# Hybrid decoder layer with a 32-expert MoE on one core: the gather reads the residual, not its normalised copy, and the router's steps are reordered

## The chip, the core and the metric

The kernel runs on one core of one Trainium2 chip. The metric is the device time of one execution in microseconds. The time before the change is the median of three runs, 1175.53 us (1170.3 to 1177.52).

## What is computed

One decoder layer over 256 positions of width 1024, all in f32: a mixer with 8 mLSTM heads and 8 attention heads, a top-4-of-32 MoE, and a gated per-layer embedding. The change touches the MoE and what stands ahead of it. Cut to that:

```python
def rmsnorm(x, g):
    return x * lax.rsqrt(jnp.mean(x * x, axis=-1, keepdims=True) + 1e-6) * g

x = x + mix @ w_out                                   # x2 in the kernel
t = rmsnorm(x, ffn_norm_g)                            # (256, 1024)
logits = t @ w_router + b_router                      # (256, 32)
top_vals, top_idx = lax.top_k(logits, 4)
gates = sum(one_hot(top_idx, 32) * softmax(top_vals)[..., None], axis=1)
for e in range(32):
    hu = t @ w_gate_up[e] + b_gate_up[e]              # 1024 -> 2 * 1024
    glu = jnp.minimum(hu[:, :1024], 7.0)
    lin = jnp.clip(hu[:, 1024:], -7.0, 7.0)
    y = y + gates[:, e:e + 1] * ((glu * sigmoid(1.702 * glu) * (lin + 1.0)) @ w_down[e] + b_down[e])
x = x + y
x = x + sigmoid(rmsnorm(x, ple_norm_g) @ w_ple_gate) * (p @ w_ple_proj)
```

## The kernel before

The kernel is one program with the order of every engine written out by hand. SP (the sync engine) issues all DMAs, PE does the matmuls, DVE, ACT and POOL the rest, and semaphores tie them together. Positions are held as two tiles `tt` of 128 rows. `xt` is the residual, 128 x 2 x 1024. A quadrant `q` is tile `q // 2`, columns `q % 2` times 512. PSUM has eight banks: `hu` (4), `po` (2) and `aux` (2).

**Weights.** They stream through `ring`, nine slots of 2 MB. `chunk_done` counts the chunks that PE has used up. Nine chunks for the mixer come first; chunk 9 of that count is the end of the output projection. The MoE then takes 192 chunks: per pair of experts 12 (`STREAM`), four of `w_gate_up` for the first expert, one for the second, two of `w_down` for the first, and so on. The first nine MoE chunks (m = 0 to 8) are loaded ahead as slots come free, m = 8 only when the router's partial products of both tiles are in PSUM (`lpart_ps`, L407). Chunk m = 9 and all later ones are refills: SP waits until PE has done chunk m - 9 (L409), and then loads 2 MB.

**From the mixer to the first gather.** PE adds the output projection in `hu`, quadrant by quadrant. DVE adds each to `xt` (`residual`, L1101), PE transposes the quadrant (L754), ACT squares it for the norm (L1441) and copies the transposed one (L1447). From these PE makes partial logits (`logit_parts`, L762), which ACT copies out (L1453), and then logits (L769). DVE routes a tile (`route_tile`, L1167 to L1178): scaled logits, the top 8, a mask of the chosen experts. PE counts positions by matmuls with the mask (L788, L790, L802), DVE turns them into slot numbers (`positions`, L1184) and a one-hot matrix of the pair's two experts with 64 slots each (L1186). `tile_h2` (L1158) writes the normalised rows h2 = xt x root x g_ffn, stored with the columns permuted. The gather multiplies h2 (the stationary operand, 128 x 128 contiguous) with the one-hot matrix into `aux` (first one: L795), and ACT copies the result to `xg` (L1473). The order of these steps on DVE is: residual 0, 1, root and h2 of tile 0, residual 2, 3, routing of tile 0, root of tile 1, positions of tile 0, h2 of tile 1, routing and positions of tile 1.

**The loop.** It runs over 16 pairs, in one pass of 64 slots where no expert has more rows. PE in a pair: first up chunk (`up_block`, L843; after its first half of k the bias, L835), scatter of the pair before in two tiles (L828, added to `xt` by DVE, L1246) between the next chunks, transposes of the gated one-hot (L900), the remaining up chunks of expert 0 and the first of expert 1, the transposes of the activation (L850), down projection (L864), three up chunks of expert 1, the gather for the next pair (L819, 16 matmuls of two passes each), transposes, down projection. DVE makes `sel`, the gated one-hot, the next one-hot (L1220) and the activations (L1260 to L1266).

**After the loop.** The last scatter, the transposes of `xt`, the gate projection (L973) and the output, which is built in `xs` (L1318, L1320). `h2` and `xs` are the same memory, `big1`.

## Time and profile before

| | |
|---|---|
| median of three runs | 1175.53 us (1170.3 to 1177.52) |
| the profiled execution, whole | 1174.7 us |
| its span, first to last instruction | 1172.6 us |
| granted TensorE clock, mean of the span | 0.989 |
| PE busy | 1124.6 us (96%) |
| DVE busy | 235.5 us (20%) |
| ACT busy | 159.9 us (14%) |
| POOL busy | 19.6 us (2%) |
| read from HBM | 429.51 MB, 367 GB/s over the span |
| chain that ended last | PE 70%, DMA 27%, DVE 1%, ACT 1% |

The profile is one execution. Times are in us from the span's start unless they are called ns. PE is the matmul side of TensorE and PEld its weight loads, which overlap it. An f32 matmul shows as two records, one per pass. The chain of work is followed back from the last instruction, each time to what released it. The granted clock is a share of 2.4 GHz. L-numbers are lines of the kernel; those of the new kernel are about 15 to 23 higher in the same place.

### The profile page before, as it was taken

What the parts mean: (1) busy time and instruction counts of PE and PEld (TensorE: products, weight loads), DVE (VectorE), ACT (ScalarE), POOL (GpSimd) and SP (SyncE); (2) the same over time, 40 slices, a digit from 0 to 9 for tenths busy, and PEclk for the clock granted to TensorE, in tenths of its full rate; (3) what the DMA queues carried; (4) which work ended last, traced back from release to release, by engine and by line L of the source; (5) the groups of instructions that cost most, each with busy time, mean ns of one, the idle gap of its engine ahead of it and who ended that gap; (6) DMA issues with size and microseconds to landing.
All of it is one profiled execution on the core that took longest, in us unless ns stands there. A gap on an engine that the chain in (4) does not pass through costs nothing.

```text
span 1172.6 us, 12150 instructions
## 1 busy us (share of the span) xinstructions
PE 1124.6 (96%) x5234; PEld 454.4 (39%) x5234; DVE 235.5 (20%) x480; ACT 159.9 (14%) x304; POOL 19.6 (2%) x44
## 2 busy tenths in 40 slices
PE   6999997999999999999999999899989998999998
PEld 3476544343434343433343333333333332424243
DVE  2364134202111111112121111111111110202021
ACT  3223312100101000000011010000000000101031
POOL 2000110000000000000000000000000000000000
PEclk9999988999999999999999999999999999999999
DMA  9932416699999999999999999999999999999950
GB/s 338 328 135 81 161 73 268 258 430 427 427 428 429 426 427 429 428 427 428 428 425 428 427 428 428 428 428 427 427 428 428 428 426 426 428 428 428 426 211 36
DMA packets 41214, 431.36 MB, mean 368 GB/s; under 512 B 5728, under 2 KB 5984, under 8 KB 16584
## 3 DMA queue, kind: packets, MB, share of 16 engines
q1 hardware_dynamic: 41160, 430.57, 87.8%
q8 instruction: 42, 0.69, 0.2%
q14 instruction: 12, 0.10, 0.0%
HBM read 429.51 MB, written 1.05 MB: 367 GB/s over the span
## 4 chain that ended last, share of the span: by engine, by line
PE 70%; DMA 27%; DVE 1%; ACT 1%; SPq 0%; issue 0%; POOL 0%; POOLq 0%; DVEq 0%; ACTq 0%
DMA ring<-in_w_gate_up 26%; PE hu L843 24%; PE po L864 14%; PE hu L542 5%; PE aux L819 5%; PE aux L828 3%; PE hu L548 2%; PE hu L557 2%; PE hu L835 2%; PE po L856 2%; PE po L973 1%; PE hu L973 1%; PE po L850 1%; PE aux L795 1%; PE po L681 0%; PE po L900 0%
## 5 line engine op out<-in xcount | busy, mean ns | idle before, releaser
L843 PE MATMUL hu<-ring,xg_t 128*64 128x512 f32 x2048 | 466.6, 597 | 22.6 <-DMA ring<-in_w_gate_up 22.6
L843 PEld LDWEIGHTS hu<-ring,xg_t 128*64 128x64 f32 x2048 | 137.7, 136 | 329.0 <-issue 284.4
L864 PE MATMUL po<-ring,early 128*64 128x512 f32 x1024 | 226.8, 595 | 0.0
L864 PEld LDWEIGHTS po<-ring,early 128*64 128x64 f32 x1024 | 70.7, 137 | 153.9 <-issue 131.4
L1260 DVE TENSOR_SCALAR early<-hu 128x512 f32<-128x512 f32 x32 | 22.1, 692 | 462.7 <-PE hu L843 462.7
L1246 DVE TENSOR_TENSOR xt<-xt,aux 128x512 f32<-128x512 f32 x68 | 43.7, 685 | 164.2 <-PE aux L828 164.2
L542 PE MATMUL hu<-ring 128*128 128x512 f32 x160 | 71.0, 597 | 0.0
L828 PE MATMUL aux<-num_t,early 64*128 64x512 f32 x272 | 67.6, 615 | 0.3 <-ACT num_t L1493 0.3
L819 PEld LDWEIGHTS aux<-early,big 128*128 128x128 f32 x512 | 58.4, 192 | 13.0 <-issue 13.0
L819 PE MATMUL aux<-early,big 128*128 128x128 f32 x512 | 61.4, 278 | 0.0
L1485 ACT ACTIVATE early<-early 128x512 f32<-128x512 f32 x32 | 20.2, 630 | 253.1 <-DVE early L1260 253.1
L1493 ACT COPY num_t<-po 128x512 f32<-128x512 f32 x32 | 18.8, 586 | 238.1 <-PE po L864 238.1
L1496 ACT COPY early<-po 128x512 f32<-128x512 f32 x16 | 9.4, 586 | 248.1 <-PE po L900 248.1
L542 PEld LDWEIGHTS hu<-ring 128*128 128x128 f32 x160 | 29.6, 190 | 34.9 <-issue 34.5
L828 PEld LDWEIGHTS aux<-num_t,early 64*128 64x128 f32 x272 | 23.5, 186 | 43.2 <-issue 42.4
L835 PE MATMUL hu<-bias,early 32*64 32x512 f32 x256 | 34.8, 613 | 0.0
L856 PE MATMUL po<-bias,early 32*64 32x512 f32 x128 | 34.4, 613 | 0.0
L557 PE MATMUL hu<-ring 128*128 128x512 f32 x64 | 33.5, 675 | 0.0
L1270 DVE COPY early<-sel_part 128x128 f32<-128x128 f32 x16 | 3.6, 228 | 142.0 <-PE po L864 140.9
L548 PE MATMUL hu<-ring 128*128 128x256 f32 x128 | 29.8, 386 | 0.0
L1489 ACT COPY early<-po 128x512 f32<-128x512 f32 x32 | 18.8, 589 | 62.6 <-PE po L850 62.6
L548 PEld LDWEIGHTS hu<-ring 128*128 128x128 f32 x128 | 23.7, 190 | 5.4 <-DVE ring L1089 1.7
(242 smaller groups left out, 549.6 us busy)
## 6 DMA issues: line engine op xcount, KB each, us to landing
ring<-in_w_gate_up SPq DMA_DIRECT2D x128, 2048.0 KB, 34.5
ring<-in_w_down SPq DMA_DIRECT2D x64, 2048.0 KB, 36.8
ring<-in_w_in SPq DMA_DIRECT2D x7, 2048.0 KB, 15.0
ring<-in_w_out SPq DMA_DIRECT2D x2, 2048.0 KB, 8.2
ring<-in_w_ple_gate SPq DMA_DIRECT2D x2, 2048.0 KB, 35.9
xt<-in_x SPq DMA_DIRECT2D x2, 512.0 KB, 4.0
ring<-in_w_ple_proj SPq DMA_DIRECT2D x1, 1024.0 KB, 33.2
out_x<-big SPq DMA_DIRECT2D x4, 256.0 KB, 2.0
```

The source lines that it names most:

```text
L542: last = mm(bank, hT[:, k, tt * P:(tt + 1) * P], slot(n, NB, K)[:, k, :], start=(k == 0), stop=(k == K - 1))
L548: last = mm(bank[:, 0:S], slot(n, NB, K)[:, k, ct * P:(ct + 1) * P], hT[:, k, :], start=(k == 0), stop=(k == K - 1))
L557: last = mm(hu[:, q, :], mixT[:, k, tt * P:(tt + 1) * P], slot(n, D, 4)[:, k % 4, b * NB:(b + 1) * NB], start=(k == 4), stop=(k == 3))
L819: last = mm(aux[:, c, (k % 4) * P:(k % 4 + 1) * P], h2[:, tt, k * P:(k + 1) * P], onehot[:, tt, :, :].rearrange("p e s -> p (e s)"), start ...
L828: last = mm(aux[:, n, :], ghotT[r, e, tt * P:(tt + 1) * P], out_s[r, e, :], start=(e == 0), stop=(e == 1))
L835: mm(hu[n * SLOTS:(n + 1) * SLOTS, 2 * e + b, :], sel[32 * b:32 * b + E, e * SLOTS:(e + 1) * SLOTS], bias[32 * b:32 * b + E, n * NB:(n + 1 ...
L843: last = mm(hu[n * SLOTS:(n + 1) * SLOTS, 2 * e + b, :], xg[:, k, e * SLOTS:(e + 1) * SLOTS], w[:, o:o + NB], start=(k == 0), stop=(k == K ...
L856: mm(po[n * SLOTS:(n + 1) * SLOTS, 0, :], sel[64:64 + E, e * SLOTS:(e + 1) * SLOTS], bias[64:64 + E, n * NB:(n + 1) * NB], start=True, sto ...
L864: last = mm(po[n * SLOTS:(n + 1) * SLOTS, 0, :], actT[:, f, h * SLOTS:(h + 1) * SLOTS], w[:, o:o + NB], start=False, stop=(h == 1 and f == ...
L973: last = mm(QUAD_BANKS[q], x3T[:, k, tt * P:(tt + 1) * P], final_slot(1 + k // 4, D, 4)[:, k % 4, n * NB:(n + 1) * NB], start=(k == 0), st ...
L1246: v.tensor_tensor(quad(xt, q), quad(xt, q), aux[:, n, :], ALU.add).then_inc(y_done, 1)
L1260: v.tensor_scalar(glu, hu[:, 2 * e, :], LIMIT, None, ALU.min).then_inc(glu_ready, 1)
```

## The change

The gather now takes `xt` itself as the stationary operand. `x_rows(tt, k)` picks every eighth column, so its 128 columns lie 8 floats apart, where h2 was read contiguously. The factor 1 / rms of each row goes into the one-hot matrix (`one_hot_tile`: one tensor_scalar per expert, compare and multiply, where one tensor_tensor did both experts), and g_ffn, now 128 x 8 in `g_perm`, is multiplied in where the gathered rows leave PSUM (`gathered`, now on DVE, 128 x 512 from PSUM, twice per pair; it was a copy on ACT). The scatter's one-hot would hold that factor too, so the gates are multiplied by the rms. `tile_h2` and the load of g_ffn over all partitions (512 KB) are gone.

The first gather writes to banks 2 and 3 of `hu`, and tile 0's half of it stands before tile 1's counting matmuls on PE. Since the gather reads `xt` in every pair, y can no longer be added there: the sums are kept in `ysum` (the memory that held h2), which POOL fills with four copies of `xt`, and the end of the kernel reads `ysum` where it read `xt`, and writes the output to `xt`.

The first refill (m = 9) is loaded in two halves, the first when PE has done the first block of chunk 0 (`first_free`). The bias matmuls of the up projection stand behind k = 2, in the second chunk, instead of behind k = 0.

```diff
-        g_ffn = sb("g_ffn", [P, D])
+        g_perm = sb("g_perm", [P, K])
...
-        h2 = xs
         hm = xs
+        ysum = xs
...
-                    sp.dma_start(g_ffn[:], ffn_norm_g.to_broadcast([P, D])).then_inc(late_loaded, 16)
+                    sp.dma_start(g_perm[:], ffn_norm_g.rearrange("o (p k) -> p (o k)", k=K)).then_inc(late_loaded, 16)
...
+                if m == RING:
+                    kind, e, part = STREAM[m]
+                    assert (kind, e) == (0, 1) and m < PER_PAIR
+                    sp.wait_ge(first_free, 1)
+                    sp.dma_start(ring[:, moe_slot(m), 0:2048], gu_src[1, part, :, 0:2048]).then_inc(first_half, 16)
+                    sp.wait_ge(chunk_done, MOE0 + 1)
+                    sp.dma_start(ring[:, moe_slot(m), 2048:4096], gu_src[1, part, :, 2048:4096])\
+                      .then_inc(ring_full[moe_slot(m)], 16)
+                    continue
...
             g.memset(ghotT, 0.0).then_inc(ghotT_ready, 1)
             g.memset(out_s, 0.0).then_inc(out_s_ready, 2)
+            for q in range(QUADS):
+                pool.wait_ge(x2_ready, q + 1)
+                g.tensor_copy(quad(ysum, q), quad(xt, q)).then_inc(y_init, 1)
...
-            def gather_part(tt, c, first):
+            def x_rows(tt, k):
+
+                return xt[:, tt, :].rearrange("p (q k) -> p k q", k=K)[:, k, :]
+
+            def first_gather(tt, c):
 
                 for k in range(4 * c, 4 * c + 4):
-                    last = mm(aux[:, c, (k % 4) * P:(k % 4 + 1) * P], h2[:, tt, k * P:(k + 1) * P],
-                              onehot[:, tt, :, :].rearrange("p e s -> p (e s)"), start=(first and k % 4 == 0), stop=not first,
+                    last = mm(hu[:, 2 + c, (k % 4) * P:(k % 4 + 1) * P], x_rows(tt, k),
+                              onehot[:, tt, :, :].rearrange("p e s -> p (e s)"), start=(tt == 0 and k % 4 == 0), stop=(tt == 1),
                               skip_group_check=True)
                 return last
 
+            pe.wait_ge(onehot_ready, 2)
+            for c in range(2):
+                first_gather(0, c)
             pe.wait_ge(mask_ready, 2)
             for b in range(2):
                 last = mm(po[:, 1, b * E:(b + 1) * E], (ones if b else before)[:], mask[:, 1, :], start=False, stop=True,
                           skip_group_check=True)
             last.then_inc(pos_ps, 1)
-            pe.wait_ge(onehot_ready, 1)
-            pe.wait_ge(xs_ready, TT + 1)
+            pe.wait_ge(onehot_ready, 4)
             for c in range(2):
-                gather_part(0, c, True)
-            pe.wait_ge(onehot_ready, 2)
-            pe.wait_ge(xs_ready, 2 * TT)
-            for c in range(2):
-                gather_part(1, c, False).then_inc(xg_ps, 1)
+                first_gather(1, c).then_inc(xg_ps, 1)
 
             def gather():
 
                 for c in range(2):
                     for k in range(4 * c, 4 * c + 4):
                         for tt in range(TT):
...
                         wait_moe_chunk(pe, ps, m)
+                        if m == RING:
+                            pe.wait_ge(first_half, 16)
                         for k in (2 * c, 2 * c + 1):
                             last = up_block(e, ring[:, moe_slot(m), :], k)
-                            if k == 0:
+                            if m == 0 and k == 0:
+                                last.then_inc(first_free, 1)
+                            if k == 2:
                                 pe.wait_ge(sel_ready, pairs + (pair + 1))
                                 up_bias(e)
                         last.then_inc(chunk_done, 1)
...
+            def one_hot_tile(tt, first):
+                for e in range(2):
+                    v.tensor_scalar(onehot[:, tt, e, :], iota_s[:], posm[:, tt, first + e:first + e + 1],
+                                    stat[:, 16 + TT + tt:17 + TT + tt], ALU.is_equal, ALU.mult).then_inc(onehot_ready, 1)
...
             residual(0)
             residual(1)
             tile_rstd(0)
-            tile_h2(0)
             residual(2)
             residual(3)
+            dve.wait_ge(lpart_ps, 1)
+            v.tensor_copy(lpart[:, 0:P], aux[:, 0, 0:P]).then_inc(lpart_ready, 1)
             route_tile(0)
             tile_rstd(1)
+            route_tile(1)
             positions(0)
-            tile_h2(1)
-            route_tile(1)
             positions(1)
 
-            def one_hot(first):
-                v.tensor_tensor(onehot, iota_s[:].rearrange("p (a b s) -> p a b s", a=1, b=1).to_broadcast([P, TT, 2, SLOTS]),
-                                posm[:, :, first].rearrange("p t (e o) -> p t e o", o=1).to_broadcast([P, TT, 2, SLOTS]),
-                                ALU.is_equal).then_inc(onehot_ready, 1)
+            def gathered(bank, count):
+
+                for c in range(2):
+                    dve.wait_ge(xg_ps, count + (c + 1))
+                    v.tensor_tensor(xg[:, 4 * c:4 * c + 4, :], bank[:, c, :].rearrange("p (k s) -> p k s", k=4),
+                                    g_perm[:, 4 * c:4 * c + 4].rearrange("p (k o) -> p k o", o=1).to_broadcast([P, 4, P]),
+                                    ALU.mult).then_inc(xg_ready, 1)
 
             routed(v.tensor_scalar(posm[:, :, E:E + 2], posm[:, :, 0:2], -float(SLOTS), None, ALU.add), False)
             routed(v.tensor_reduce(cnt[:, 0:1], po[:, 1, E:2 * E], AX.X, ALU.max), False)
...
+            gathered(hu[:, 2:4, :], 0)
...
-                v.tensor_scalar(gates[:, tt, :], gates[:, tt, :], stat[:, 36 + tt:37 + tt], None, ALU.mult)\
-                 .then_inc(gates_ready, 1)
+                v.tensor_scalar(gates[:, tt, :], gates[:, tt, :], stat[:, 36 + tt:37 + tt],
+                                stat[:, 8 + TT + tt:9 + TT + tt], ALU.mult, ALU.mult).then_inc(gates_ready, 1)
             dve.wait_ge(gates_ready, TT)
+            dve.wait_ge(y_init, QUADS)
...
-                    v.tensor_tensor(quad(xt, q), quad(xt, q), aux[:, n, :], ALU.add).then_inc(y_done, 1)
+                    v.tensor_tensor(quad(ysum, q), quad(ysum, q), aux[:, n, :], ALU.add).then_inc(y_done, 1)
...
                     activation(1)
-
-                dve.wait_ge(onehot_ready, pairs + (PAIRS + 2))
+                    gathered(aux[:], ps * (2 * PAIRS) + (2 * pair + 2))
...
-            def logit_rows(tt):
-
-                act.wait_ge(lpart_ps, tt + 1)
-                a.copy(lpart[:, tt * P:(tt + 1) * P], aux[:, tt, 0:P]).then_inc(lpart_ready, 1)
-
-            for q in range(QUADS):
+            for q in range(2):
                 act.wait_ge(x2_ready, q + 1)
-                quad_squares(q, 24 + q, junk)
-                if q == 1:
-                    root(TT, stat[:, 2:3], True)
-                if q == 3:
-                    logit_rows(0)
+                quad_squares(xt, q, 24 + q, junk)
+            root(TT, stat[:, 2:3], True)
+            for q in range(2):
+                quad_columns_x2(q)
+            for q in range(2, QUADS):
+                act.wait_ge(x2_ready, q + 1)
+                quad_squares(xt, q, 24 + q, junk)
                 quad_columns_x2(q)
             root(TT + 1, stat[:, 3:4], True)
-            logit_rows(1)
+            act.wait_ge(lpart_ps, 2)
+            a.copy(lpart[:, P:S], aux[:, 1, 0:P]).then_inc(lpart_ready, 1)
             for tt in range(TT):
                 act.wait_ge(negtop_ready, tt + 1)
                 a.activation(gates[:, tt, :], lg[:, tt, :], ACT.Exp, bias=stat[:, 32 + tt:33 + tt]).then_inc(route_exp, 1)
 
-            def gathered(count):
-
-                for c in range(2):
-                    act.wait_ge(xg_ps, count + (c + 1))
-                    a.copy(xg[:, 4 * c:4 * c + 4, :].rearrange("p k s -> p (k s)"), aux[:, c, :]).then_inc(xg_ready, 1)
-
-            gathered(0)
...
-                    gathered(ps * (2 * PAIRS) + (2 * pair + 2))
```

DVE, from the end of tile 0's routing to the logits of tile 1 (`lg`), `mask` and `posm` are the chosen experts and slot numbers, `big` is h2. Before:

```order
L1172 CAST topf<-topi 128x8
L1173 TENSOR_TENSOR early<-iota_e,topf 128x128
L1177 TENSOR_REDUCE mask<-early 128x32
L1178 TENSOR_SCALAR stat<-top 128x1
L1153 TENSOR_TENSOR stat<-stat 128x1
L986 RECIPROCAL stat<-stat 128x1
L1184 SCALAR_TENSOR_TENSOR posm<-po,mask 128x32
L1186 TENSOR_TENSOR early<-iota_s,posm 128x128
L1158 SCALAR_TENSOR_TENSOR big<-xt,stat,g_ffn 128x128x8
L1167 SCALAR_TENSOR_TENSOR lg<-aux,stat,brb 128x32
L1170 MAX top<-lg 128x8
L1171 MAX_INDEX topi<-top,lg 128x8
```

Now, from the same place; `early<-iota_s,posm,stat` is the one-hot with the root in it:

```order
L1174 TENSOR_TENSOR stat<-stat 128x1
L1007 RECIPROCAL stat<-stat 128x1
L1180 SCALAR_TENSOR_TENSOR lg<-aux,stat,brb 128x32
L1183 MAX top<-lg 128x8
L1184 MAX_INDEX topi<-top,lg 128x8
L1185 CAST topf<-topi 128x8
L1186 TENSOR_TENSOR early<-iota_e,topf 128x128
L1190 TENSOR_REDUCE mask<-early 128x32
L1191 TENSOR_SCALAR stat<-top 128x1
L1202 SCALAR_TENSOR_TENSOR posm<-po,mask 128x32
L1195 TENSOR_SCALAR early<-iota_s,posm,stat 128x64 x2
L1202 SCALAR_TENSOR_TENSOR posm<-po,mask 128x32
```

The second h2 has gone from between, and positions of tile 0 moved from ahead of tile 1's routing to behind it.

PE, from the last logits to the first gather; `po` rows are the counting matmuls, L795 the gather of both tiles. Before:

```order
L762 MATMUL aux<-ring,w_r 32x128 x8
L769 MATMUL aux<-sel_part,early 128x32
L788 MATMUL po<-mask,before 128x32
L790 MATMUL po<-mask,ones 128x32 x2
L802 MATMUL po<-mask,before 128x32
L802 MATMUL po<-mask,ones 128x32
L795 MATMUL aux<-early,big 128x128 x16
```

Now; L814 is the gather, into `hu`:

```order
L777 MATMUL aux<-ring,w_r 32x128 x8
L784 MATMUL aux<-sel_part,early 128x32
L803 MATMUL po<-mask,before 128x32
L805 MATMUL po<-mask,ones 128x32 x2
L814 MATMUL hu<-early,xt 128x128 x8
L824 MATMUL po<-mask,before 128x32
L824 MATMUL po<-mask,ones 128x32
L814 MATMUL hu<-early,xt 128x128 x8
```

Tile 0's eight gather matmuls moved ahead of tile 1's two counting ones (L824).

ACT, from the first square of the residual on (`early,stat<-xt` is a square, `ring<-hu` the copy of a transposed quadrant, `stat<-stat` a root, `early<-aux` the copy of partial logits). Before:

```order
L1441 ACTIVATE early,stat<-xt 128x512
L1447 COPY ring<-hu 128x4x128
L1441 ACTIVATE early,stat<-xt 128x512
L1331 ACTIVATE stat<-stat,eps_t 128x1
L1447 COPY ring<-hu 128x4x128
L1441 ACTIVATE early,stat<-xt 128x512
L1447 COPY ring<-hu 128x4x128
L1441 ACTIVATE early,stat<-xt 128x512
L1453 COPY early<-aux 128x128
L1447 COPY ring<-hu 128x4x128
L1331 ACTIVATE stat<-stat,eps_t 128x1
L1453 COPY early<-aux 128x128
```

Now:

```order
L1464 ACTIVATE early,stat<-xt 128x512 x2
L1354 ACTIVATE stat<-stat,eps_t 128x1
L1470 COPY ring<-hu 128x4x128 x2
L1464 ACTIVATE early,stat<-xt 128x512
L1470 COPY ring<-hu 128x4x128
L1464 ACTIVATE early,stat<-xt 128x512
L1470 COPY ring<-hu 128x4x128
L1354 ACTIVATE stat<-stat,eps_t 128x1
L1485 COPY early<-aux 128x128
```

The second square and the root moved ahead of the first copy, and the copy of tile 0's partial logits left ACT for DVE.

## Rows read from the trace of the kernel before

**Rows 1.** Page: GB/s in 40 slices of 29.3 us each.
```profile
GB/s 338 328 135 81 161 73 268 258 430 427 427 428 429 426 427 429 428 427 428 428 425 428 427 428 428 428 428 427 427 428 428 428 426 426 428 428 428 426 211 36
```

**Rows 2.** Windows: us, busy PE PEld DVE ACT POOL, clock, DMA, GB/s.
```profile
200.00:210.00 10.00, 8.93 (x44) 7.73 (x44) 4.43 (x23) 2.03 (x4) 0.00 (x0) 0.61 0.18 74
210.00:220.00 10.00, 10.00 (x48) 3.13 (x48) 1.28 (x2) 0.75 (x1) 0.00 (x0) 1.00 0.65 228
...
400.00:1100.00 700.00, 680.13 (x3350) 246.26 (x3352) 110.89 (x192) 63.74 (x109) 0.00 (x0) 1.00 1.01 427
```

**Rows 3.** Chain in order of time: start, length, what.
```profile
208.51 1.87 PE hu L843 x8
...
264.30 1.72 PE hu L843 x8
...
658.47 38.11 DMA ring<-in_w_gate_up
...
1072.28 38.43 DMA ring<-in_w_gate_up
...
1119.65 7.04 PE po L864 x32
```

**Rows 4.** Timeline of the DMA queue (SP): the first refills.
```profile
213.30 0.33 SPq L398 DMA_DIRECT2D ring<-in_w_gate_up  x1
218.80 0.33 SPq L398 DMA_DIRECT2D ring<-in_w_down  x1
224.30 0.33 SPq L398 DMA_DIRECT2D ring<-in_w_down  x1
228.47 0.33 SPq L398 DMA_DIRECT2D ring<-in_w_gate_up  x1
```

**Rows 5.** Timeline of the routing and first gather, PE, DVE and ACT.
```profile
186.37 1.88 PE L557 MATMUL hu<-ring 128*128 128x512 f32 x4
...
189.93 1.26 DVE L1101 TENSOR_TENSOR xt<-xt,hu 128x512 f32<-128x512 f32 x2
...
192.92 0.26 ACT L1453 COPY early<-aux 128x128 f32<-128x128 f32 x1
...
194.14 0.25 DVE L1167 SCALAR_TENSOR_TENSOR lg<-aux,stat,brb 128x32 f32<-128x32 f32 x1 [2.94 <-PE aux L769]
...
195.74 0.15 DVE L1153 TENSOR_TENSOR stat<-stat 128x1 f32<-128x1 f32 x1
...
196.13 0.25 ACT L1453 COPY early<-aux 128x128 f32<-128x128 f32 x1
...
199.40 0.23 DVE L1167 SCALAR_TENSOR_TENSOR lg<-aux,stat,brb 128x32 f32<-128x32 f32 x1
...
201.07 0.63 PE L802 MATMUL po<-mask,before 128*128 128x32 f32 x2 [3.56 <-DVE mask L1177]
...
201.94 6.56 PE L795 MATMUL aux<-early,big 128*128 128x128 f32 x32
...
202.39 0.29 DVE L1186 TENSOR_TENSOR early<-iota_s,posm 128x128 f32<-128x128 f32 x1
```

**Rows 6.** Timeline: POOL, product of two operands from SBUF.
```profile
164.55 1.04 POOL L488 TENSOR_TENSOR big<-big 128x512 f32<-128x512 f32 x1 [1.92 <-DVE big L1130]
```

**Rows 7.** PEld groups by line; timeline of PE for the same lines.
```profile
L819 PEld LDWEIGHTS aux<-early,big 128*128 128x128 f32 x512 | 58.4, 192 | 13.0 <-issue 13.0
...
L850 PEld LDWEIGHTS po<-ident,early 128*128 128x128 f32 x128 | 17.9, 207 | 13.0 <-issue 13.0
...
L900 PEld LDWEIGHTS po<-ident,early 128*128 128x128 f32 x64 | 6.7, 141 | 13.0 <-issue 13.0
```

**Rows 8.** Timeline of PE: transposes L900, gather L819, transposes L850.
```profile
224.19 0.66 PE L900 MATMUL po<-ident,early 128*128 128x128 f32 x4
...
251.97 3.84 PE L819 MATMUL aux<-early,big 128*128 128x128 f32 x32
...
255.64 0.64 PE L850 MATMUL po<-ident,early 128*128 128x128 f32 x4
```

More of the change, by code:

```diff
@@ L265, in hybrid_layer @@
         ghot_ready = sem("ghot_ready")
+        y_init = sem("y_init")
+        first_free = sem("first_free")
+        first_half = sem("first_half")
         ghotT_ps = sem("ghotT_ps")
@@ L427, in _ @@
                 sp.wait_ge(fin_step, 2 * q + 2)
-                sp.dma_start(quad(out_dst, q), quad(xs, q)).then_inc(stored, 16)
+                sp.dma_start(quad(out_dst, q), quad(xt, q)).then_inc(stored, 16)
             sp.wait_ge(stored, 16 * TT * HALVES)
@@ L749, in _, with quad_transposes @@
             w_out_part(3, range(0, 2))
-            def quad_transposes(q, bank):
+            def quad_transposes(src, q, bank):
                 for j in range(4):
-                    last = tr(bank[:, j * P:(j + 1) * P], quad(xt, q)[:, j * P:(j + 1) * P], ident[:])
+                    last = tr(bank[:, j * P:(j + 1) * P], quad(src, q)[:, j * P:(j + 1) * P], ident[:])
                 last.then_inc(xq_ps, 1)
@@ L780, in _ @@
             pe.wait_ge(x2_ready, 4)
-            quad_transposes(3, hu[:, 3, :])
+            quad_transposes(xt, 3, hu[:, 3, :])
             logits(0)
@@ L818, in gather @@
                         for tt in range(TT):
-                            last = mm(aux[:, c, (k % 4) * P:(k % 4 + 1) * P], h2[:, tt, k * P:(k + 1) * P],
+                            last = mm(aux[:, c, (k % 4) * P:(k % 4 + 1) * P], x_rows(tt, k),
                                       onehot[:, tt, :, :].rearrange("p e s -> p (e s)"), start=(tt == 0), stop=(tt == TT - 1))
@@ L916, in _ @@
                         up_chunk(1, c, m0 + 6 + c)
-                    pe.wait_ge(onehot_ready, pairs + (pair + 3))
+                    pe.wait_ge(onehot_ready, ps * (4 * PAIRS) + (4 * pair + 8))
                     pe.wait_ge(y_done, ps * (QUADS * PAIRS) + (pair * QUADS + 4))
@@ L1154, in tile_rstd @@
                 rstd(TT + tt)
-            def tile_h2(tt):
-                v.scalar_tensor_tensor(out=h2[:, tt, :].rearrange("p (k q) -> p q k", k=K),
-                                       in0=xt[:, tt, :].rearrange("p (q k) -> p q k", k=K),
-                                       scalar=stat[:, 16 + TT + tt:17 + TT + tt],
-                                       in1=g_ffn[:].rearrange("p (q k) -> p q k", k=K),
-                                       op0=ALU.mult, op1=ALU.mult).then_inc(xs_ready, 1)
             def route_tile(tt):
@@ L1271, in _ @@
                                   .rearrange("p (e o) -> p e o", o=1).to_broadcast([P, 2, SLOTS])).then_inc(sel_ready, 1)
-                    dve.wait_ge(onehot_ready, pairs + (pair + 2))
+                    dve.wait_ge(onehot_ready, ps * (4 * PAIRS) + (4 * pair + 4))
                     for tt in range(TT):
@@ L1281, in _ @@
                     dve.wait_ge(xg_ps, ps * (2 * PAIRS) + (2 * pair + 2))
-                    one_hot(slice(2 * pair + 2, 2 * pair + 4))
+                    for tt in range(TT):
+                        one_hot_tile(tt, 2 * pair + 2)
                     for tt in range(TT):
@@ L1436, in _, with quad_squares @@
             output_tile(1)
-            def quad_squares(q, col, buf):
+            def quad_squares(src, q, col, buf):
                 act.wait_ge(ss_ready, TT + col - 24)
-                a.activation(buf, quad(xt, q), ACT.Square, accum_out=stat[:, col:col + 1]).then_inc(ss_ready, 1)
+                a.activation(buf, quad(src, q), ACT.Square, accum_out=stat[:, col:col + 1]).then_inc(ss_ready, 1)
             def quad_columns_x2(q):
```

17 lines of the change are left out of this document (8 added, 9 removed).

## The prediction

> **What bounds the kernel now.** I read the page's slices first, then the busy time by stretch, then the chain of work in order of time. From about 235 us to 1125 us the core moves 425 to 430 GB/s in every slice [rows 1]. Between 400 and 1100 us the DMA engines are busy all the time (share 1.01, 427 GB/s), while PE has 680 of 700 us [rows 2]. Between 200 and 210 us the same engines move 74 GB/s: the nine slots of the ring are full, and nothing has been consumed yet.
>
> The chain has two regimes [rows 3]. An expert pair begins with a group of L843. The first pair begins at 208.51 and the second at 264.30, 55.8 us later. From 658.5 on each pair of the chain has about 38 us of the DMA of w_gate_up; from the first such piece (658.47) to the last (1072.28) there are seven pairs, 59.12 us each. A pair loads 12 chunks of 2.097 MB, 25.17 MB, and 25.17 MB / 427 GB/s = 58.9 us: the later pairs are the DMA's rate. PE alone would be through sixteen pairs at 208.5 + 16 x 55.8 = 1101.3; the last pair's down projection ends at 1126.7. So PE has 25.4 us of slack over the whole loop, 1.59 us per pair. The end is set by the time at which the DMA stream becomes continuous, plus the bytes after it, plus a tail on PE.
>
> **When the stream becomes continuous.** The refills are issued at 213.30, 218.80, 224.30 and 228.47 [rows 4], each when PE frees a chunk. In 210 to 220 us 2.28 MB arrived [rows 2], 5.3 us of work at 427 GB/s, so bytes begin near 214.7, 1.4 us after the issue. A refill takes 4.9 us. The first ends at 219.6, the second runs from 220.2 to 225.1, the third from 225.7 to 230.6; the fourth, ready at 229.9, is the first that finds the queue busy. The third refill sets everything after it, and it is issued 224.30 - 208.50 = 15.8 us after the first gather's end (201.94 + 6.56 [rows 5]), with PE busy throughout. What the change is worth is how far it moves that gather's end, as long as PE's own pair stays under about 57.4 us.
>
> **The route before the first gather.** Its steps stand in [rows 5]. I take the new order from the rows of the two orders above and the old durations.
> 1. residual(2) and (3) ran at 189.93, behind h2(0) on DVE. Quadrants 0 and 1 are now squared back to back on ACT, the root comes earlier, and h2 is gone; residual(3) then waits only for the last w_out part (PE 186.37 + 1.88 = 188.25) and ends near 189.0, 2.2 us earlier.
> 2. ACT copied quadrant 1 late, behind a root; both copies of tile 0 now come before the third square. The router's parts of tile 0 can run at 188.8 and end by 189.9 even at the slow clock. DVE instead of ACT copies them. From the old copy (192.92) to the old L1167 (194.14) it was 1.22 us: new L1180 at 191.1.
> 3. L1167 to the sum L1153 was 1.60 us: the sum of tile 1 at 192.7, ACT's copy of its router rows 0.39 us later at 193.1, L1180 of tile 1 1.22 us later at 194.3. From 199.40 to PE's L802 at 201.07 it was 1.67 us: mask of tile 1 at 196.0 instead of 201.07. The second h2, which stood between, is gone.
> 4. New: positions(0) stands behind this. The one-hot took 0.29 us (202.39) and posm ahead of it somewhat less, 0.5 together; the one-hot is now two instructions, so I give it 0.15 more: PE can begin tile 0's gather at 196.7. Its 16 passes take 16 x 0.205 = 3.3 us (6.56 / 32), and now stand ahead of tile 1's counting matmuls: 200.0. From L802 to the one-hot's end it was 202.39 + 0.29 - 201.07 = 1.61 us, with the split 1.75: gather of tile 1 from 201.8.
> 5. That gather takes 3.3 us at the slow clock or 16 x 0.12 = 1.9 at the fast one; the old one ran nearly whole at 1.2 GHz (granted 0.61 over 200 to 210 us [rows 2]). End between 203.7 and 205.1; I take 204.6. The multiplication by g_perm on DVE starts when half of it is done and costs a PSUM add's 0.63 us (189.93, two in 1.26): ready near 204.0, so just hidden. Without that cover it would cost up to 0.7 us.
>
> Gather end 208.5 to 204.6: **3.9 us**.
>
> **The other edits.** The refill in halves: the first half leaves after one block, some 2.9 us earlier relative to the gather, but the second refill still waits for chunk 1, whose release stays about 10.3 us behind the gather, so the DMA engines only idle at another place. Nothing. The bias matmuls moved behind k = 2 take one microsecond out of chunk 0 and put it in chunk 1; chunk 2 is where it was. Nothing. The dropped 512 KB of g_ffn were loaded while the DMA engines had gaps. Nothing. In the loop DVE gets two multiplications (1.3 us) and two more one-hot instructions per pair, all while PE has its 7 us of down projection, so nothing; if they were exposed at the pair's start it would be at most 1.4 us of the 1.59 us of slack. The sum in its own buffer costs four copies on POOL. The nearest row is POOL's product of the same size, 1.04 us [rows 6]; four of them from 189.8 end by 194, long before y is touched. But they overlap tile 0's routing on DVE. The trace has no DVE instruction with two SBUF inputs beside a POOL one that reads. Bounds: 0, or two DVE instructions each waiting out one copy, 2.1 us. I take 0.4.
>
> By the Trainium skill (SBUF, the section on the engine ports) a DVE instruction with two SBUF inputs and a GpSimd one that reads SBUF exclude each other for a whole instruction. By that rule the dearer bound is the likelier one; no row here shows it.
>
> **The strided gather.** h2 was stored permuted and read contiguously; x_rows reads xt with a step of 8 floats as the stationary operand, in every pair. No row shows it for an ordinary f32 matmul. A pass of the gather loads its weights in 192 ns and they are hidden (3.84 us for 32 in a warm pair, 0.12 each [rows 7, 8]). The one strided load is in L850, the transposes of glu with a step of 4: 207 ns against 141 ns for L900, unstrided. Lower bound 0: the load stays hidden. Upper bound: the 66 ns come in full on each pass, 32 x 0.066 = 2.1 us per pair. I take 10 ns, since the neighbouring row's own load still fits beside its matmul: 0.3 us per pair, inside the slack, but paid once in the tail, where the last gather is on the chain. Plus 0.3 us.
>
> Sum: 3.9 - 0.4 - 0.3 = 3.2 us. The profiled execution took 1174.7 us (span 1172.6), and 1174.7 - 3.2 = 1171.5. The median of the runs shown is 1175.5, 0.8 above; I put the forecast between, at **1172 us**. A measurement of this kernel can tell about 1% (11.7 us) from no change; this is 0.3%.
>
> **Rivals.**
> A. *The strided weights make PE the bound* (slower). If a pass's load is no longer hidden, the cost is 32 d per pair for d of excess. The slack is used up at 25.4 / 512 = 50 ns; the end is 1% later at (25.4 + 3.5 + 11.7) / 512 = 79 ns. At the 66 ns bound: 33.8 - 25.4 - 3.5 = +4.9, 1180 us. If the excess were the whole of a 258 ns load less the 0.12 us pitch, 138 ns: 70.7 - 25.4 - 3.5 = +41.8, 1217 us. For it: L850's 66 ns, already above the turning point of 50. Against it: four L850 transposes take 0.64 us, the four unstrided ones of L900 0.66, so the longer load was hidden [rows 8], and an ordinary load (192 ns) is already slower than a transpose's (141), so that it may have room for the step. 14 in 100, 10 of them beyond 1%.
> The Trainium skill (SBUF, the note on cachelines) says that f32 reads with steps beyond four elements touch a new 16-byte line each time and pay for it. By that rule alone the gather would be dearer; whether it is dearer than what is hidden it doesn't say. L850's row agrees with a price for the step.
> B. *The gain on the route goes elsewhere.* Tile 0's gather holds PE while tile 1's mask waits, the copies on POOL stop DVE for 2.1 us, and the new g_perm step is exposed by 0.7: gather end 207.4, gain about 1, less the tail: 1174 us. 11 in 100.
> C. *The clock is up in the first gather* and both halves run at 2.4 GHz: 1.4 us less for tile 0, 0.9 for tile 1, and earlier counts; gather end 202.3, 1169 us. Against: the granted clock around the old one. 8 in 100.
> D. *The halved refill or the earlier bias gives more*, because the fourth to sixth refill, not the third, set the stream; chunk releases behind an earlier bias come 1 us sooner, 1168 to 1171 us. 5 in 100.
>
> The forecast itself (1169.5 to 1173.5) has 62 in 100. Nearly all cases lie inside 1%: faster 2, same 87, slower 11. The range adds what runs differ by (1170.3 to 1177.5 before): 1167 to 1178, which leaves out A's dear part and a little of B and C.
>
> **What would show it.** In the profile after: the first L860 near 204.6; refills issued near 207, 214.3 and 219.6 in place of 213.3, 218.8, 224.3; a pair of 55.6 to 56.2 us early and 59.1 late; gather's loads (L836) near 192 ns with 32 in under 4.2 us. Wrong are: loads of 300 ns there and no DMA waits in the chain (A); DVE gaps between L1180 and L1190 while POOL copies (B); a first refill that moves the end although the third stands still (D).

## The result: 3% slower, and the profile after

The changed kernel takes 1210.25 us (median of 4; 1208.17 to 1210.68) against 1174.18 us for the kernel before (4 runs). The ratio is 1.0301, interval 1.0277 to 1.0324. The profiled execution's span is 1208.5 us against 1172.6. The prediction was 1172 us, range 1167 to 1178. It was wrong: it argued for a gain of 3 us, and the change costs 36.

The page of the kernel after, as [rows 1] of before: PE's total, the GB/s of the 40 slices (30.2 us each) and the chain by engine.
```profile
PE 1185.0 (98%) x5234; PEld 522.1 (43%) x5234; DVE 265.9 (22%) x563; ACT 141.2 (12%) x269; POOL 21.8 (2%) x48
...
GB/s 332 297 140 70 207 80 210 359 420 424 417 424 421 425 421 426 420 425 420 423 420 424 419 424 422 426 420 424 421 425 419 427 419 424 424 425 420 283 1 35
...
PE 97%; DVE 1%; ACT 1%; SPq 0%; DMA 0%; POOL 0%; issue 0%; POOLq 0%; DVEq 0%; ACTq 0%
```

DMA has gone from the chain (0%); in [rows 3] it stood there from 658 us on, with 38 us of each pair. The busy time by stretch says the same (us, busy PE PEld DVE ACT POOL, clock, DMA share, GB/s). PE now has all of the 700 us, at full granted clock, where [rows 2] had 680.13, and the DMA engines move 423 GB/s where they moved 427:
```profile
200.00:400.00 200.00, 199.14 (x916) 83.20 (x917) 41.80 (x91) 15.13 (x23) 0.00 (x0) 0.99 0.94 390
400.00:1100.00 700.00, 700.00 (x3240) 288.79 (x3238) 129.73 (x242) 49.66 (x83) 0.00 (x0) 1.00 1.00 423
```

The chain of the kernel after in order of time (start, length, what). The first line is the first pair's first group behind the gather, as the 208.51 of [rows 3]:
```profile
206.72 4.34 PE hu L860 x16
...
251.01 7.85 PE aux L836 x32
...
310.73 7.81 PE aux L836 x32
...
370.41 7.81 PE aux L836 x32
...
1146.24 7.81 PE aux L836 x32
```
From 310.73 to 370.41 a pair takes 59.68 us. The sum 206.7 + 16 x 59.68 = 1161.6 is 1.0 us short of the end of the last down projection at 1162.6: the first pair is that much longer, since its first group above took 4.34 us (at a granted clock of 0.50, that is 1.2 GHz, until about 208 us) where later pairs have 3.43. Before, PE alone needed 55.8 us for the first pair and 55.65 for the next ones, and the DMA stream gave 59.12. The chain of the kernel before, two pairs in a row ahead of the first DMA wait:
```profile
585.91 3.77 PE aux L819 x32
...
641.56 3.77 PE aux L819 x32
```
The four microseconds from 55.65 to 59.68 are in one group of 32 matmuls, the gather: 7.81 us where before had 3.77 (3.84 in the first pair, [rows 8]).

The groups by line (busy us, mean ns of one | idle before) show what is in those 32 passes. The first row answers to L819 of [rows 7], the third to L850 and the fourth to L900:
```profile
L836 PEld LDWEIGHTS aux<-early,xt 128*128 128x128 f32 x512 | 123.1, 334 | 13.0 <-issue 13.0
L836 PE MATMUL aux<-early,xt 128*128 128x128 f32 x512 | 126.1, 405 | 0.0
...
L867 PEld LDWEIGHTS po<-ident,early 128*128 128x128 f32 x128 | 19.8, 220 | 13.0 <-issue 13.0
...
L921 PEld LDWEIGHTS po<-ident,early 128*128 128x128 f32 x64 | 6.7, 140 | 13.0 <-issue 13.0
```
A pass's weight load, now with a step of 8 floats, takes 334 ns instead of 192, and the pitch of the passes is 7.81 / 32 = 0.244 us instead of 0.12. Of the 142 ns that the load grew by, 126 come out in the pitch.

The route before the gather did become shorter. The timeline of the kernel after (start us, us, engine, line, operation [idle before <- releaser]):
```profile
189.21 0.69 DVE L1122 TENSOR_TENSOR xt<-xt,hu 128x512 f32<-128x512 f32 x1 [1.83 <-PE hu L572]
...
190.59 2.28 POOL L525 COPY big<-xt 128x512 f32<-128x512 f32 x4
...
191.04 0.25 DVE L1180 SCALAR_TENSOR_TENSOR lg<-aux,stat,brb 128x32 f32<-128x32 f32 x1 [0.50 <-PE aux L784]
...
191.85 0.49 DVE L1185 CAST topf<-topi 128x8 f32<-128x8 uint32 x1
192.37 0.64 DVE L1186 TENSOR_TENSOR early<-iota_e,topf 128x128 f32<-128x128 f32 x1
...
194.51 0.25 DVE L1180 SCALAR_TENSOR_TENSOR lg<-aux,stat,brb 128x32 f32<-128x32 f32 x1 [0.53 <-PE aux L784]
...
195.33 0.17 DVE L1185 CAST topf<-topi 128x8 f32<-128x8 uint32 x1
195.53 0.29 DVE L1186 TENSOR_TENSOR early<-iota_e,topf 128x128 f32<-128x128 f32 x1
...
196.93 4.19 PE L814 MATMUL hu<-early,xt 128*128 128x128 f32 x16 [1.52 <-DVE early L1195]
...
202.53 4.18 PE L814 MATMUL hu<-early,xt 128*128 128x128 f32 x16 [0.86 <-DVE early L1195]
...
209.39 0.33 SPq L409 DMA_DIRECT2D ring<-in_w_gate_up  x1
...
211.11 0.33 SPq L411 DMA_DIRECT2D ring<-in_w_gate_up  x1
```
The logits of both tiles come when the prediction said (191.04 and 194.51; forecast 191.1 and 194.3), and the first gather ends at 206.7, 1.8 us earlier than before, not 3.9. The mixer was later in this execution: PE's last w_out part ended at 189.2 us (187.28 + 1.88), before at 188.25. Counted from there the route is 2.7 us shorter. The third refill of the ring (L401, the second of w_down) is issued at 223.3 us instead of 224.3 [rows 4]. It no longer matters: PE is late, not the data.

### The profile page after: what moved, and what is told of

Read it like the earlier page. It is cut to its first block, busy times and chain, and to the rows that moved or that the text cites. A ratio compares the mean times of both kernels' runs of the same rounds, so it can differ in the third digit from the quotient of the medians.

```text
span 1208.5 us, 12233 instructions
## 1 busy us (share of the span) xinstructions
PE 1185.0 (98%) x5234; PEld 522.1 (43%) x5234; DVE 265.9 (22%) x563; ACT 141.2 (12%) x269; POOL 21.8 (2%) x48
## 4 chain that ended last, share of the span: by engine, by line
PE 97%; DVE 1%; ACT 1%; SPq 0%; DMA 0%; POOL 0%; issue 0%; POOLq 0%; DVEq 0%; ACTq 0%
PE hu L860 37%; PE po L881 19%; PE aux L836 10%; PE aux L845 5%; PE hu L557 5%; PE hu L852 3%; PE po L873 3%; PE hu L572 3%; PE hu L563 2%; PE po L867 2%; PE po L994 1%; PE hu L994 1%; PE po L921 1%; PE hu L814 1%; PE po L696 0%; SPq L379 0%
## 5 line engine op out<-in xcount | busy, mean ns | idle before, releaser
L836 PEld LDWEIGHTS aux<-early,xt 128*128 128x128 f32 x512 | 123.1, 334 | 13.0 <-issue 13.0
L836 PE MATMUL aux<-early,xt 128*128 128x128 f32 x512 | 126.1, 405 | 0.0
L1267 DVE TENSOR_TENSOR big<-big,aux 128x512 f32<-128x512 f32 x68 | 43.7, 684 | 152.1 <-PE aux L845 152.1
L557 PEld LDWEIGHTS hu<-ring 128*128 128x128 f32 x160 | 29.6, 190 | 34.9 <-issue 34.5
L1239 DVE TENSOR_TENSOR xg_t<-aux,g_perm 128x512 f32<-128x512 f32 x32 | 22.1, 691 | 67.8 <-PE aux L836 67.8
```

The source lines that it names most:

```text
L557: last = mm(bank, hT[:, k, tt * P:(tt + 1) * P], slot(n, NB, K)[:, k, :], start=(k == 0), stop=(k == K - 1))
L836: last = mm(aux[:, c, (k % 4) * P:(k % 4 + 1) * P], x_rows(tt, k), onehot[:, tt, :, :].rearrange("p e s -> p (e s)"), start=(tt == 0), sto ...
L1267: v.tensor_tensor(quad(ysum, q), quad(ysum, q), aux[:, n, :], ALU.add).then_inc(y_done, 1)
```

## The experiments

The theory: the step in the weights' address makes a load longer than what the matmuls beside it hide, in every pair, so that PE needs more than the DMA's 59.1 us; all the rest of the change is a gain of a few microseconds. The main rival: the loss comes from the rest of the change, that is the new buffer with its copies, the new order, the refills or the multiplication by g_perm. Within the theory two forms stand against each other: the price grows with the step, or it is one per 16 bytes touched, so that a step of 2 floats costs nothing and 4 as much as 8.

### The step alone, taken out and put in

Out of the changed kernel:
```diff
             def x_rows(tt, k):
-                return xt[:, tt, :].rearrange("p (q k) -> p k q", k=K)[:, k, :]
+                return xt[:, tt, k * P:(k + 1) * P]
```


> The changed kernel with the gather reading 128 neighbouring columns instead of every eighth one; so it gathers other columns than it should, the rest is the same. If the step of 8 floats in the weight load is the whole loss (theory S), a pass of the gather goes back from 0.245 to 0.12 us, a pair to 55.7 us at first and 59 us later, and the whole to 1170 to 1173 us. If the loss is in the other parts of the loop, the factor in the one-hot matrix or the evacuation on DVE (theory R), the passes stay at 0.245 us and the time at 1205 to 1212 us.

Measured: 1171.53 us (6 runs), ratio 0.9962 (0.9942 to 0.9981). Groups by line, and the chain of this kernel:
```profile
L836 PEld LDWEIGHTS aux<-early,xt 128*128 128x128 f32 x512 | 58.4, 192 | 13.0 <-issue 13.0
...
L836 PE MATMUL aux<-early,xt 128*128 128x128 f32 x512 | 61.4, 278 | 0.0
```
```profile
653.93 39.31 DMA ring<-in_w_gate_up
696.94 3.77 PE aux L836 x32
...
1067.95 39.46 DMA ring<-in_w_gate_up
1111.11 3.77 PE aux L836 x32
```
The load is back at 192 ns, the gather at 3.77 us, and the DMA is back in the chain, from 654 us on as in [rows 3]. This kernel gathers other columns than it should, but its instructions are otherwise those of the changed one. All the rest of the change together is a gain of 0.4%, 4.5 us.

Into the kernel before, with nothing else of the change: h2 is written in natural order, and the gather reads it with the step.
```diff
-last = mm(aux[...], h2[:, tt, k * P:(k + 1) * P],
+last = mm(aux[...], h2[:, tt, :].rearrange("p (q k) -> p k q", k=K)[:, k, :],
...
-v.scalar_tensor_tensor(out=h2[:, tt, :].rearrange("p (k q) -> p q k", k=K), ...
+v.scalar_tensor_tensor(out=h2[:, tt, :], in0=xt[:, tt, :], ..., in1=g_ffn[:],
```


> The kernel before, with h2 stored in its natural column order and read by the gather with the step of 8 floats; nothing else is changed. Theory S: the load of a pass takes 334 ns, the pair 59.7 us, and the time is 16 x 4.0 - 27.7 = 36 us above that of before, less 1.5 us for h2's write in order: 1207 to 1211 us. Theory R: 1172 to 1176 us.

Measured: 1213.47 us, ratio 1.0323 (1.0305 to 1.034). Its groups by line and its busy time by stretch:
```profile
L819 PEld LDWEIGHTS aux<-early,big 128*128 128x128 f32 x512 | 123.1, 334 | 13.0 <-issue 13.0
```
```profile
400.00:1100.00 700.00, 700.00 (x3240) 288.75 (x3238) 108.28 (x186) 62.68 (x107) 0.00 (x0) 1.00 1.00 422
```
The step alone turns the old kernel into one bound by PE, and costs as much as the whole change (the intervals 1.0305 to 1.034 and 1.0277 to 1.0324 overlap). The time lies 2.5 us above the range that was expected; 1.3 of it can be the first gather, which that range left out and which takes 7.86 us here instead of 6.56. The buffer, the order, the refills and g_perm are not in this kernel: as causes of the loss they fall.

### From which step on

In the changed kernel, with smaller steps (4, then 2; step 4 shown):
```diff
-return xt[:, tt, :].rearrange("p (q k) -> p k q", k=K)[:, k, :]
+return xt[:, tt, (k // 4) * 4 * P:(k // 4 + 1) * 4 * P].rearrange("p (q s) -> p s q", s=4)[:, k % 4, :]
```


> The changed kernel with a step of 4 floats in the gather (other columns than it should gather). If the price is for each new line of 16 bytes that a load touches (theory L), step 4 costs as much as step 8: loads of 334 ns, passes of 0.245 us, 1210 us. If it grows with the distance (theory D), the load is near 240 to 260 ns, the pass 0.16 to 0.18, and the pair is bound by the DMA again: 1172 to 1180 us.

> The changed kernel with a step of 2 floats in the gather (other columns than it should gather). Theory L: two floats of each 16-byte line are used, so the load is between 192 and 250 ns and mostly hidden: 1170 to 1178 us. Theory D: load near 210 ns, the same time. If any step costs the full price: 334 ns and 1210 us.

Measured: step 4 takes 1207.95 us (2 runs), ratio 1.0276 (1.0256 to 1.0297); step 2 takes 1171.13 us, ratio 0.996 (0.9937 to 0.9983). The groups by line, step 4 and then step 2, and the gather of step 2 in the chain:
```profile
L836 PEld LDWEIGHTS aux<-early,xt 128*128 128x128 f32 x512 | 120.7, 328 | 13.0 <-issue 13.0
```
```profile
L836 PEld LDWEIGHTS aux<-early,xt 128*128 128x128 f32 x512 | 61.5, 196 | 13.0 <-issue 13.0
```
```profile
1110.51 3.97 PE aux L836 x32
```
It is a cliff, not a slope: contiguous 192 ns, step 2 196, step 4 328, step 8 334. The gather of a pair takes 3.77, 3.97, 7.67 and 7.81 us. Step 2 costs 0.2 us a pair, which the slack takes up. The cliff lies between a step of 2 and of 4 floats, as theory L says: two floats per 16 bytes do nearly as well as four, one does not. A bound on the distance between 8 and 16 bytes would look the same; no run has a step of 3 or a stretch that starts elsewhere in a line. The Trainium skill (SBUF — State Buffer, the note on cachelines) says that an access wants at least two hits in a 16-byte line and that a new line on each access is penalised. By that rule 2 is free and 4 and 8 are alike; the runs agree within the 0.2 us of step 2 and the 0.14 between 4 and 8. The same note's figure of four fp32 as a step that is free doesn't hold here: step 4 pays nearly all.

### How much more a pair may take

The turning point of rival A (1.59 us per pair) was worked out from rows of one kernel. Here contiguous passes are added to the kernel before, by redoing some of the gather's blocks (shown for 6; 3 is alike):
```diff
-for k in range(4 * c, 4 * c + 4):
+for k in ([*range(4 * c, 4 * c + 4)] + [*range(4 * c, 4 * c + (6 + 1 - c) // 2)]):
```


> The kernel before; PE does 3 of the gather's 8 column blocks twice in each pair (same result), 12 contiguous passes more, 1.4 us per pair. By the prediction's slack of 1.59 us per pair the DMA stays the bound, and only the last gather's 1.4 us shows: 0 to 3 us above before. If the loss of the change had nothing to do with PE's slack, nothing is told by this run and the next.

> The kernel before; PE does 6 of the 8 column blocks twice, 24 passes more, 2.8 us per pair. A pair is then 58.5 us for PE, still less than the DMA's 59.1, but by the slack over the whole loop (25.4 to 27.7 us) 16 x 2.8 = 45 us is too much: PE is the bound throughout, 17 to 20 us above before. If a pair only had to stay under the DMA's 59.1 us: 0 to 5 us above before.

Measured: 12 passes more, 1.34 us per pair, ratio 1.0005 (0.9994 to 1.0017). 24 passes more, 2.68 us per pair, ratio 1.0119 (1.01 to 1.0139), about 14 us. The chain with 12 more, then with 24 more:
```profile
896.19 36.97 DMA ring<-in_w_gate_up
936.86 5.11 PE aux L819 x44
...
1073.11 37.80 DMA ring<-in_w_gate_up
1114.60 5.11 PE aux L819 x44
```
```profile
254.11 6.45 PE aux L819 x56
...
312.44 6.45 PE aux L819 x56
...
1129.01 6.45 PE aux L819 x56
```
With 12 more the DMA enters the chain only for the last four pairs, at 896 us instead of 658: most of the slack is used, and no loss can be measured. With 24 more a pair takes 58.33 us on PE, still 0.8 us less than the stream's 59.12, and yet the kernel loses. The chain shows no DMA wait in any pair: PE would have to use up the chunks loaded ahead before the stream sets the end, and at 58.33 us a pair it never does. By the prediction's formula the loss would be 16 x 2.68 - 25.4 = 17.5 us, and 17 to 20 us were expected; it is 14 (11.8 to 16.3). With the 55.65 us of the later pairs the slack is 27.6 us (1126.69 - 264.30 - 15 x 55.65), and the formula gives 15.3, inside the interval.

### The copies on POOL

In the kernel without the step (the first one above, which gathers other columns), the copies wait until both one-hots are done:
```diff
-pool.wait_ge(x2_ready, q + 1)
+pool.wait_ge(onehot_ready, 4)
```


> The changed kernel with neighbouring columns in the gather (other columns than it should gather), and POOL's four copies only after the last one-hot of the first pair. If POOL's copies held up DVE in tile 0's routing (port theory), CAST L1185 and TENSOR_TENSOR L1186 of tile 0 take 0.17 and 0.29 us as for tile 1, instead of 0.49 and 0.64, and the gather ends 0.7 us earlier relative to the first residual; if the longer durations have another cause, they stay.

Measured: 1171.26 us, ratio 0.9984 (0.9965 to 1.0003). The timeline of this kernel, tile 0's two instructions and the copies:
```profile
190.62 0.17 DVE L1185 CAST topf<-topi 128x8 f32<-128x8 uint32 x1
190.82 0.29 DVE L1186 TENSOR_TENSOR early<-iota_e,topf 128x128 f32<-128x128 f32 x1
...
200.38 2.28 POOL L525 COPY big<-xt 128x512 f32<-128x512 f32 x4 [10.97 <-DVE early L1195]
```
In the kernel after, tile 0's L1185 and L1186 took 0.49 and 0.64 us while the copies ran, and tile 1's 0.17 and 0.29 behind them. With the copies late, tile 0's take 0.17 and 0.29 too. So the copies hold up these two DVE instructions, 0.32 + 0.35 = 0.67 us in all, and from the start of residual(3) to the start of tile 0's gather it is 7.07 us instead of the 7.74 of the kernel with early copies. L1183 (MAX8, one input) took 0.20 us beside the copies and behind them. By the Trainium skill (SBUF — State Buffer, the section on who interferes with whom) a DVE instruction with two SBUF inputs and a GpSimd one that reads SBUF exclude each other; L1186, with two inputs, agrees. The time of the whole kernel doesn't show the 0.67 us: the interval overlaps that of the kernel with early copies.

### Versions that keep the gain

First, the permutation is done in the copy that POOL makes anyway: xp is the copy of x2 in the order in which h2 was stored, the gather reads it contiguously, and the sums stay in xt.
```diff
-g.tensor_copy(quad(ysum, q), quad(xt, q)).then_inc(y_init, 1)
+tt, n = divmod(q, HALVES)
+g.tensor_copy(xp[:, tt, :].rearrange("p (k q) -> p k q", k=K)
+              [:, :, n * (P // 2):(n + 1) * (P // 2)],
+              quad(xt, q).rearrange("p (q k) -> p k q", k=K)).then_inc(y_init, 1)
...
-return xt[:, tt, :].rearrange("p (q k) -> p k q", k=K)[:, k, :]
+return xp[:, tt, k * P:(k + 1) * P]
```


> The changed kernel with the roles of the two buffers exchanged: POOL writes the copy of x2 with its columns permuted, the gather reads that copy contiguously, and the sums stay in xt. The root in the one-hot matrix, g_perm on DVE and the refill in halves are kept. Theory S with L (each new line of 16 bytes is what costs, and nothing else was lost): loads of 192 ns, passes of 0.12 us, 1169 to 1173 us, or 0.993 to 0.998 of before. If POOL's permuted copies (read with a step of 8) come late, tile 0's gather waits for the second and tile 1's for the fourth: 1 to 3 us later. Theory R: above 1200 us.

The second leaves the first refill whole, the third has tile 1's counting matmuls ahead of tile 0's gather again; both are the first one otherwise.

> The run before this one, with the first refill (m = 9) in one piece again. By the prediction's step that the third refill sets the stream: same time within 0.3 us, with the second and third refill issued at the same distance from the gather's end. By rival D the half is worth something: 1 to 3 us slower.

> As the run with the permuted copy, with tile 1's counting matmuls on PE ahead of tile 0's gather again, tile 1's part of the gather directly behind tile 0's. If tile 0's gather held up tile 1's one-hot (rival B), the gather ends 1.0 to 1.5 us earlier and so does the whole: 1168 to 1172 us. If not, no change.

Measured, 12 runs each (11 of them in the first ratio): 1171.67 us, ratio 0.9978 (0.9967 to 0.999); whole refill 1172.67 us, 0.9996 (0.9982 to 1.001); counts first 1171.95 us, 0.9981 (0.9964 to 0.9998). The first and the third are the fastest kernels found here that compute all, 0.2% below before, and can't be told apart. In the third one's trace the time from residual(3) to the end of the gather is 14.6 us instead of 16.1, as much as was expected, but 0.4 of it is in the passes themselves (5.05 us for 32, against 3.41 + 2.05), and the whole is not faster. The timeline of the first, with the copies, three instructions of tile 0's routing and the first gather:
```profile
188.03 4.29 POOL L526 COPY big<-xt 128x512 f32<-128x512 f32 x4
...
189.29 0.92 DVE L1189 CAST topf<-topi 128x8 f32<-128x8 uint32 x1
190.25 1.12 DVE L1190 TENSOR_TENSOR early<-iota_e,topf 128x128 f32<-128x128 f32 x1
...
191.67 0.67 DVE L1178 TENSOR_TENSOR stat<-stat 128x1 f32<-128x1 f32 x1
...
196.04 3.41 PE L816 MATMUL hu<-early,big 128*128 128x128 f32 x16 [1.25 <-DVE early L1199]
...
200.68 2.05 PE L816 MATMUL hu<-early,big 128*128 128x128 f32 x16 [0.85 <-DVE early L1199]
```
The four copies now take 4.29 us instead of 2.28, and the three DVE instructions beside them 0.92, 1.12 and 0.67 us where they take 0.17, 0.29 and 0.15 alone: 2.1 us, three times what the plain copies cost the route. From residual(3) to tile 0's gather it is 9.4 us instead of 7.7. So this version pays for its permutation on the route, and only the step is got rid of.

Whether the halved refill is worth anything stays open. The two ratios lie 2.1 us apart, inside the 1 to 3 us of rival D and not within the 0.3 us of the other expectation, but their intervals overlap. The traces speak for nothing: of the 6.1 us between the profiled executions, 4.7 lie ahead of residual(3) (186.65 and 191.39 us) and 2.4 in the first gather (granted clock over 200 to 210 us: 1.00 and 0.50), where no refill can act, and behind it the kernel with the whole refill is 1 us shorter. The distance from the gather's end to the third refill is 15.8 to 16.0 us in both.

Last, a version without any permutation: w_gate_up is loaded so that partition p holds rows p, 128 + p, and so on, in two pieces of 8 KB per partition instead of one of 16 KB; late copies, counts first.
```diff
-gu_src = w_gate_up[0].rearrange("e (p c k) n -> e c p (k n)", c=4, k=2)
+gu_src = w_gate_up[0].rearrange("e (c k p) n -> e c p k n", c=4, k=2)
```


> The changed kernel without any column permutation: the gather reads 128 neighbouring columns of xt, and w_gate_up is loaded in that row order, so that each DMA moves 2 x 8 KB per partition instead of 16 KB in a piece; the norm's weights come from cols. POOL's copies stand after the last one-hot, and the counting matmuls of tile 1 stand before tile 0's gather. If 8 KB pieces move at the same 427 GB/s: gather end 1.5 to 2 us earlier than in the run with neighbouring columns alone, 1167 to 1171 us, 0.992 to 0.997 of before. If they are slower by 1%, the loop gets 9 us longer: 1177 us or more, with fewer GB/s between 400 and 1100 us.

Measured: 1178.51 us, ratio 1.0015 (0.9998 to 1.0032). It also takes the norm's weights from another tile. Its third refill goes out at 217.2 us, 7.1 us before that of the kernel before and the earliest of all, and still it is no faster, as the expectation's second case had it. Its busy time by stretch:
```profile
400.00:1100.00 700.00, 673.17 (x3302) 241.43 (x3300) 133.10 (x252) 50.24 (x84) 0.00 (x0) 1.00 1.01 423
```
The DMA engines are never idle (1.01), PE has slack, and the rate is 423 GB/s instead of 427. Over some 950 us of stream that is 950 x 4 / 427 = 9 us, more than the 7.1 gained; from the third refill to the end of the span it takes 959.0 us instead of 948.3. The layout of the pieces is the only thing that differs in these loads, so it is the likely reason, but no run varies it alone.

## Why the prediction was wrong, step by step

- **What bounds the kernel, and the slack.** Right in kind, the slack 2.2 us too small: 55.8 us is the first pair's time, the later ones take 55.65, which makes it 27.6. Rival A's formula with the measured excess of (7.81 - 3.77) / 32 = 0.126 us per pass, 4.04 us per pair, gives 64.6 - 25.4 - 3.5 = +35.7: 1174.7 + 35.7 = 1210.4 us, where 1210.25 were measured. That it fits so well is luck, because two errors cancel: the slack is too small, and the gain ahead of the loop was 1.8 us in this kernel, not 3.5. From the two traces it is 64.6 - 27.6 - 1.8 + 0.8 = 36.0 us (the 0.8 is what the first pair's slow start adds), and the spans differ by 35.9.
- **The strided gather: the step that failed.** The term "I take 10 ns, since the neighbouring row's own load still fits beside its matmul" was some 12 times too small, and even its upper bound, 66 ns from L850, was half of the truth. L850 misled twice. Its load grew by 66 ns from a base of 141 (a transpose), while an ordinary f32 load starts at 192 and grew by 142. And its four transposes follow each other every 0.16 us and hid the longer load, while the gather's passes follow each other every 0.12 us: of the 142 ns, 126 came out. The row that was near in the program was not near in what decides, how long the load is against the pitch. Rival A was named, with its turning point (50 ns), its sign (loads of 300 ns, no DMA in the chain) and a case at 138 ns worth 1217 us; it had 14 in 100. The one row that bore on it stood above the turning point, and the rule of the Trainium skill cited there (SBUF — State Buffer, the note on cachelines) spoke for it: as the runs show, rightly.
- **The route before the first gather.** The times fit, logits at 191.04 and 194.51 (191.1 and 194.3) and tile 0's gather from 196.93 (196.7), but in part by luck. The forecast starts from the end of the last w_out part at 188.25 us, which came 0.9 us later in this execution: residual(3) ended at 189.9, not "near 189.0". From there to tile 0's logits it took 1.9 us, not 2.85, and to tile 0's gather 7.8, not 8.45. Wrong is what the gather itself takes: 4.19 and 4.18 us for 16 passes instead of 3.3 and 2.8. Only a part of that is the step. Without it the trace has
```profile
196.29 3.78 PE L814 MATMUL hu<-early,xt 128*128 128x128 f32 x16 [1.87 <-DVE early L1195]
```
at a granted clock of 0.50, 0.236 us a pass. The 0.205 of the forecast was a mean over 32 passes, the last of which, from about 207.7 us on, ran at 1.00. Without the step the up projection begins at 205.06, and with the copies late at 204.1, on either side of the forecast 204.6.
- **The sum of the other terms.** 3.9 - 0.4 = 3.5 us forecast, 4.5 measured without the step (interval 2.2 to 6.8). Right, but the size is known only roughly: with a step of 2 it is 4.7 us, with the copies late 1.9 (-0.4 to 4.1), with the permuted copies 2.6 (1.2 to 3.9).
- **The copies on POOL.** 0.4 taken, 0.67 seen in the trace between the bounds 0 and 2.1. Right in kind. The upper bound was met by the permuted copies (2.1 us).
- **"The third refill sets everything after it."** The span less the third refill's issue is 948.3 us before ([rows 4]: 1172.6 - 224.30), and 948.4, 949.4, 949.9, 948.6, 950.4 and 948.1 in the six kernels of the change whose weights are contiguous or of step 2 and whose loads are as before. Right within 2.1 us, with a third refill issued anywhere from 218.6 to 226.0. The second to fourth refill keep their distance in all of these kernels, so that no run tells which of them it is. In the list of signs the third refill stands at 219.6; 224.3 less the forecast gain of 3.9 is 220.4, and 220.9 was measured without the step.
- **Refill in halves, bias, g_perm.** Nothing forecast. What the halves are worth is open (ratios 2.1 us apart, nothing in the traces); bias and g_perm have no run of their own, but lie within the few microseconds above.

## What to carry to other kernels

When an operand of a matmul moves from contiguous to strided, its weight load must be priced against the pitch of that very group of matmuls, not against another group's: where 32 passes already run at 0.12 us each, 126 of 142 ns were exposed, and that is paid in every iteration. A step of 2 floats cost 0.2 us a pair here, one of 4 almost as much as one of 8, 3.9 and 4.0 us. If a copy is made anyway, it can do the permutation, but look at what it runs beside: the slower copy held up DVE for 2.1 us. A loop that waits for DMA has less room than its steady state shows (59.12 - 55.65 = 3.5 us a pair here): 2.7 us a pair more on PE already cost 14 us, because PE never used up the chunks loaded ahead; take the slack over the whole loop (27.6 us, 1.7 a pair). And a mean over a stretch in which the granted clock changes is no price at either level.

## What was unexpected in the hardware

- The load of 128 x 128 f32 weights takes 192 ns contiguous, 196 ns with a step of 2 floats, 328 with 4 and 334 with 8. A pass of the gather (128 columns) goes from 0.12 us to 0.124, 0.240 and 0.244. In the transposes of L850 and L867 a step of 4 gives 207 to 220 ns against 141.
- A pass with a step of 8 hardly feels the clock: the 16 of tile 0 in the first gather took 4.19 us at a granted clock of 0.50 (197 to 201 us), 0.26 each, and they take 0.244 at 1.00. Contiguous ones took 3.78 us at 0.50, 0.236 each, and 0.12 at 1.00.
- A copy of 128 x 512 f32 on POOL takes 0.57 us, and 1.07 when it reads with a step of 8 floats. While the copies run, a DVE cast of 8 columns waits as well (0.49 and 0.92 us instead of 0.17), not only an instruction with two inputs, and so does one with two inputs of a single column (0.67 instead of 0.15).
